# Two transformer blocks in one kernel: all steps of the stage beside a weight group stand behind the slot's last block

## What is computed

```python
# first block
proj = rms_norm(x, norm1_g) @ w_in            # q, k, v of two attentions, input of the convolution branch, gates
out_a = window_attention(qa, ka, va, sink_a)  # 8 heads of 64, window of 128 tokens to each side
out_b = hyena_branch(hy_in, ...)              # short convolution, generated filters, two long convolutions
out_c = diff_attention(qc, kc, vc, lam)       # 4 heads, two softmaxes each, their difference
merged = g0 * (out_a @ w_oa) + g1 * (out_b @ w_ob) + g2 * (out_c @ w_oc)
x = x + merged @ w_out
x = x + (silu(h2 @ ffn_w1) * (h2 @ ffn_w3)) @ ffn_w2
# second block
o = concat(rmsnorm(fox_attention(...)), rmsnorm(stick_breaking_attention(...)))   # 8 heads each
x = x + o @ w_out_2
x = x + (silu(gate) * val) @ w_down_2         # gate, val from a projection with a short convolution
return rmsnorm(x, final_norm_g)
```

## Time and profile before

| what | value |
| --- | --- |
| median of 3 runs | 1744.34 us (1743.65 to 1744.95) |
| the profiled execution's own time | 1748.23 us |
| its span, from the first to the last instruction | 1746.4 us |
| busy: TensorE, VectorE, ScalarE, GpSimd | 96%, 48%, 38%, 16% |
| mean granted TensorE clock | 0.985 |
| HBM traffic over the span | 79 GB/s |

### The profile page before, as it was taken

The page is one execution under the profiler, slowest core; times in us unless marked ns, Lnnn a source line. Parts: engine busy times, 40 slices in busy tenths (PEclk is TensorE's granted clock), DMA queues, the critical chain, the costliest instruction groups (busy, mean ns, idle before and its releaser), DMA issues.

```text
span 1746.4 us, 19135 instructions
## 1 busy us (share of the span) xinstructions
PE 1677.4 (96%) x7584; PEld 1316.7 (75%) x7584; DVE 834.1 (48%) x1330; ACT 659.9 (38%) x1150; POOL 272.5 (16%) x280
## 2 busy tenths in 40 slices
PE   5999999999999999999999998999999999999997
PEld 3557787777766787888888877776678788888886
DVE  5445455465356454333332224366654466666323
ACT  4332123454344433333332223455564344444221
POOL 3453305461012111000000002013210100000001
PEclk9999999999999999999999998999999999999999
DMA  6111112212121232332333322311101233233331
GB/s 225 61 61 48 49 53 86 71 49 61 60 62 48 99 107 73 97 97 97 96 97 96 97 84 65 102 60 36 37 25 61 73 97 97 97 97 97 109 97 72
DMA packets 39222, 139.51 MB, mean 80 GB/s; under 512 B 4332, under 2 KB 4972, under 8 KB 38941
## 3 DMA queue, kind: packets, MB, share of 16 engines
q1 hardware_dynamic: 39132, 138.29, 24.3%
HBM read 136.14 MB, written 2.10 MB: 79 GB/s over the span
## 4 chain that ended last, share of the span: by engine, by line
PE 87%; DVE 5%; POOL 3%; ACT 3%; issue 2%; DMA 0%; DVEq 0%; POOLq 0%; SPq 0%; ACTq 0%
PE ps L346 84%; PE ps L349 3%; ACT whi L1347 1%; POOL small L1801 1%; POOL small L1807 1%; DMA x<-in_x 0%; DVE wlo L778 0%; DVE W L1189 0%; POOL small L1804 0%; ACT junk L1359 0%; DVE st L1050 0%; DVE xs L789 0%; DVE sd L869 0%; DVE uT L922 0%; DVE uT L920 0%
## 5 line engine op out<-in xcount | busy, mean ns | idle before, releaser
L778 DVE TENSOR_TENSOR wlo<-wraw,whi 128x1024 fp32r<-128x1024 f32 (+2 forms) x220 | 267.1, 1215 | 523.9 <-ACT whi L1347 523.8
L346 PE MATMUL ps<-hThi,whi 128*128 128x512 f32 x1128 | 455.3, 404 | 2.2 <-DVE hTlo L794 1.3
L1347 ACT ACTIVATE whi<-wraw 128x1024 fp32r<-128x1024 f32 (+2 forms) x244 | 252.8, 1037 | 504.0 <-PE ps L346 498.5
L346 PE MATMUL ps<-hTlo,whi 128*128 128x512 f32 x1128 | 441.9, 392 | 0.0
L346 PE MATMUL ps<-hThi,wlo 128*128 128x512 f32 x1128 | 441.6, 392 | 0.0
L346 PEld LDWEIGHTS ps<-hThi,whi 128*128 128x128 f32 x1128 | 213.7, 189 | 58.1 <-issue 16.0
L346 PEld LDWEIGHTS ps<-hThi,wlo 128*128 128x128 f32 x1128 | 213.3, 189 | 45.7
L346 PEld LDWEIGHTS ps<-hTlo,whi 128*128 128x128 f32 x1128 | 213.7, 189 | 44.3 <-issue 2.9
L346 PE MATMUL ps<-whi,achi 128*128 128x512 f32 x352 | 136.9, 389 | 0.0
L346 PE MATMUL ps<-wlo,achi 128*128 128x512 f32 x352 | 136.9, 389 | 0.0
L346 PE MATMUL ps<-whi,aclo 128*128 128x512 f32 x352 | 136.9, 389 | 0.0
(11 more groups left out here) (270 smaller groups left out, 2199.1 us busy)
## 6 DMA issues: line engine op xcount, KB each, us to landing
wraw<-in_ws SPq DMA_DIRECT2D x236, 512.0 KB, 3.5
x<-in_x SPq DMA_DIRECT2D x4, 512.0 KB, 7.7
x<-in_x SPq DMA_DIRECT2D x1, 2048.0 KB, 8.2
out<-xs SPq DMA_DIRECT2D x8, 256.0 KB, 2.0
dec<-in_dec SPq DMA_DIRECT2D x1, 1024.0 KB, 15.2
wraw<-in_ws SPq DMA_DIRECT2D x4, 256.0 KB, 2.5
vec<-in_vec SPq DMA_DIRECT2D x1, 788.0 KB, 4.6
w<-in_w SPq DMA_DIRECT2D x1, 512.0 KB, 13.6
```

Of the source, the lines that this page charges most:

```text
L346: return t.matmul(o, l, r, start=first, stop=last)
L778: v.tensor_tensor(wlo[h][:, 0:width(i)], wraw[h][:, 0:width(i)], whi[h][:, 0:width(i)].bitcast(F32), ALU.subtract).then_inc(lo_done[h], 1)
L1347: a.activation(whi[h][:, 0:width(i)], wraw[h][:, 0:width(i)], ACT.Copy).then_inc(hi_done[h], 1)
```

## The change

In `slots`, which all four compute engines' programs share, the steps that stood behind a block other than the last now stand behind the last block, together with the slot's last step and after `flow.tick()`. How many steps a slot has doesn't change, nor their order, nor their content. Groups of rate 1 keep the same program.

```diff
             split(first + s + 1 + LA)
             for b in range(nb):
                 yield s, b, s == n_s - 1
-                if b < nb - 1:
-                    flow.pump((b + 1) * rate // nb - b * rate // nb)
             flow.tick()
-            flow.pump(rate - (nb - 1) * rate // nb)
+            flow.pump(rate)
```

## The result

The changed kernel takes 1795.86 us (median of 4 runs, 1795.25 to 1797.01). The kernel before took 1744.64 us beside it (4 runs, 1743.65 to 1750.69). The ratio is 1.0288, 95% interval 1.0274 to 1.0303: slower by 51 us. A ratio given here is an estimate from all the runs measured side by side, with its 95% interval in brackets, and differs a little from the quotient of two medians (1.0294 here). Three executions in all, one of the kernel before (2109 us) and two of the last experiment (3110 and 3374 us), ran in a slower state and are left out of every ratio.

The account below looks back on a forecast made before the run. TensorE, busy 96% of the span, bounds the kernel. Terms 10.1 + 0 + 12.4 + 10 + 9 = 41.5 us on 1748.2 give 1789.7, median 3.9 lower: 1785; forecast 1775 to 1800 (0.60), low 1762, high 1808.

Parts of the forecast that it names:

- Filters and hyena, waits: Filters and hyena stage: new TensorE waits at step 2, filter taps and back transforms, +10.1 us in sum.
- Step 2: Second step of the filters, directly behind step 1: its wait grows from 1.40 to 4.43 us, +3.0.
- the back transforms: Hyena pairs 23-24 and 33-34: wait for GpSimd's last sum, 2.8 us each, before 0.1 and 0.5.
- Window: Window stage: end-slot waits stand against saved matmul changes; sum 0, between -2 and +2 us.
- The rotary rival: ScalarE and VectorE leave end slots of `qc`, `kc` late, so more steps wait: 15 to 25 us on top; chance 0.20.
- Differential, waits: Differential stage: second steps wait for the first's answers, 20.7 us new, 8.3 of old idle time returned, net +12.4.
- The 2.9: Differential pair 2-3: first step has no values, so the second waits 4.58 - 1.68 = 2.9 us.
- The two of 2.85: Differential pairs 8-9 and 12-13: second step's `turn` waits for bank 6 back from `out`, 2.85 us each.
- Stick, waits: Stick stage: `fq` pairs and bursts of four steps in `fk`, `fv` wait 19.4 us, less 7.3 and 2: +10.
- The clock: TensorE's granted clock drops behind waits of about 2 us or more, 1.3 us each: 16 waits, a difference of +9 us.
- The rival that the clock holds: New waits leave TensorE at 2.4 GHz and today's 6.7 us loss goes too: +26 us, 1770; chance 0.15.
- the one that the doubled cover wins: Doubled cover before first steps decides, 22 us come back; with 10 us of waits 1732; chance 0.03.

Follow-up runs that it names:

- the last experiment: Kernel before with `out`, `low`, `high` a step later, `combine` before `highest` on VectorE, and window steps behind each slot's second block: 1743.1 us, ratio 0.9977.
- The single slot: Kernel before with the change only in slot 0 of `hy0`, putting step 2 directly behind step 1: 1753.53 us, ratio 1.0040.

## Why the prediction was right, and where its terms were off

The forecast was 1785 us, with 1775 to 1800 for its own case, and 1795.9 was measured. The mechanism is as told: second steps of a pair wait for what they lost the cover of, and the clock adds to it. The sum of 41.5 us stands against 47.2 between the profiled executions, and against 51 between the medians. That it came so near is in part luck: the stick waits were put some 7 us too high and the rest of the program came out 3.4 us lower, which hid more than half of the 17 us by which the clock was put too low. The measured values below are those of the two profiled executions, and they add up to the 47.2 (10.6 - 0.3 + 11.0 + 3 + 26.3 - 3.4).

- **Filters and hyena, waits: +10.1, measured +10.6.** Step 2 waited 4.35 us where 4.43 was worked out, the back transforms 3.19 and 2.65 where 2.8 each was, pair 7-8 of the taps 1.98 where 1.6 was. The single slot confirms the first of them by itself. The small waits of the other taps nearly all stayed out (one of 0.31).
- **Window: 0, measured -0.3**, with 1.3 us more idle and 1.6 less busy. Taken alone it measured +0.25%: the waits of its end slots can bring the clock down, which the prediction didn't count. The rotary rival's 15 to 25 us are ruled out: the waits for ScalarE's `qcT` and `kcT` grew from 1.6 to 2.2 us together.
- **Differential, waits: 20.7 new less 8.3 old = +12.4, measured +11.0.** The answer came when it was worked out: in pair 4-5 the transposition starts 4.59 us after the first step did (539.65 to 544.24), against 4.58. The wait was 1.85 and not 2.0 because the trace counts TensorE busy for 2.75 us of it; the prediction said 2.58, and its own working, 512.31 plus eight of 0.11, gives 2.46. The 2.9 was 2.94. The two of 2.85 were 2.54, with the answer 5.67 us after the start and not 5.85. Pair 0-1 waited 1.84 where 2.7 was worked out: its first product needs bank 4 alone, which is free when the first exponential ends, 2.97 us after the start, and not when both do. Pair 16-17 waited 0.76 where 1.4 was. That the waits for `ocs` would go was right but for one of 0.5.
- **Stick, waits: 19.4 less 7.3 less 2 = +10, measured about +3** (5.0 more idle, less the 2 for saved changes). This term was too large. `fq` waits 2.75 us (3.0 predicted), but the bursts add up to 9.5 and not 16.4: the two with the norm 3.4 and 3.2 where 5.4 and 5.1 stood, the five others 2.9 together where 5.9 stood. The burst was followed through with TensorE's steps at full speed, and it was at half speed in most of the two large ones, so it came later to what it needed. That this is the reason is argued; with two pairs in place of a burst, at a higher clock, the wait for the norm (`olo`) was one of 3.3 us, which fits.
- **The clock: +9, measured +24.3** (busy time in filters, differential and stick, 6.9 + 7.5 + 10.0, with the saved changes still in it; some 26.3 with stick's 2 us for them added back). This is the term that was mis-sized: "I take 16 and a difference of +9", at 1.3 us for each wait from about 2 us on. The number of waits was right: the trace has 13 of 1.84 us or more in these stages, four in filters and hyena, eight in differential, one in stick (and one of 1.74). The price for one was too low where the wait is long or followed by steps that wait again: 3.0 us behind the single wait of 4.35, about 12 in stick (10.0 and the 2 saved), where only 1.74 and 2.09 us are waits of that size. How much it is also differs by kernel: in the runs with one stage changed the same three stages' busy time grew by 5.6, 1.6 and 10.0 us, 17 in all. The bursts were sized as single waits, by the rows for one wait, since the trace of before has no burst.
- **The rest of the program: 0, measured -3.4.** It has the same instructions; its busy time is 4.2 us less and its idle time 0.8 us more.

The rival that the clock holds is ruled out, as is the one that the doubled cover wins. The rule of the Trainium skill that the prediction named ("TensorE: Matmul & The Clock Gate", "Why this matters for your kernels") would have made the clock nearly free. For the one wait that it did warn of, the 4.35 us in front of step 2, the trace agrees with it: the busy time grew by 3.0 us. For the rest it disagrees with these traces, where the granted clock fell behind waits of 1.84, 1.85 and 1.98 us. What decides whether it falls behind a given wait isn't settled: in differential it fell behind the wait of 2.94 us in one kernel and not behind that of 2.93 in another, and in the kernel after not behind either of 2.54. The first row has the 24 weight matmuls behind pair 0-1, whose wait was 1.84, at 0.70; the second those behind a wait of 2.54, at full clock:

```profile
516.42:524.14 7.72, 7.72 (x25) 6.14 (x25) 5.16 (x10) 2.19 (x5) 2.96 (x3) 0.70 0.21 68
...
576.46:582.02 5.56, 5.56 (x28) 4.54 (x27) 3.16 (x8) 2.51 (x5) 0.00 (x0) 1.00 0.10 20
```

## What to carry to other kernels

Small steps that depend on each other are worth most when work of the length of the other engines' answer stands between them: read that length (here 4.6 us for a step of differential) from the trace, and count cover gap by gap, because cover added in front of one step doesn't pay for cover taken from in front of the next. Price the clock beside each wait: here a wait of about 2 us was followed by anything from no loss to 2.2 us of slower weight matmuls (7.72 in place of 5.56 us behind the one of 1.84), one of 4.35 by 3.0 us, and two bursts of dependent steps lost 6.8 us in busy time for 1.1 us more idle. That share differed by several us from one kernel to the next. Where a single wait stands out, moving its one consumer a step later, as for `out`, is the cheaper remedy than moving everything.

## What the runs showed of the hardware that was not expected

- The same instructions with nearly the same waits ran at different clocks in different kernels: differential 141.15 us at 0.92 and 135.57 at 0.96 with 19.3 and 19.5 us idle, window 176.51 at 1.00 and 179.56 at 0.98 with 2.97 and 2.95 us idle, untouched `sq` 50.14 at 1.00, 51.89 at 0.96 and 52.98 at 0.94. A difference of some 3 us in one stage is no evidence on an edit elsewhere unless the clock is read beside it.
- Runs of one kernel differ in the same way: the kernel before took 1743.0 us at a mean clock of 0.990 and 1748.1 at 0.983. The clock goes with much of its spread, not with all: 1749.6 us came at 0.986.
- More idle time can go with less total time (two pairs in place of a burst: 1.0 us more idle, 3.0 us shorter), and so can more work (40 matmuls more, 6.9 us shorter in the stage than after, and 1.3 us shorter than with differential alone).
